# The first attention in batches of four heads, with p turned by block moves and VectorE instead of TensorE

## The reference: what is computed

```
h = rmsnorm(x, g_pre)
q, k, v, z = split(h @ w_in_a)
s = q k^T * scale + slope * distance          # masked to the window
p = exp(s - m) ; denominator = sum(p) + exp(sink - m)
o = p v / denominator
x = x + rmsnorm((o * silu(z)) @ w_out_a, g_post)
...
sh1, sc1, gt1, sh2, sc2, gt2 = silu(c) @ w_ada + b_ada
```

## Time and profile before

| | |
|---|---|
| median of 3 runs | 1768.04 us (1767.06 to 1768.81) |
| the profiled execution | 1767.72 us, its span 1766.0 us |
| TensorE busy | 1754.1 us, 99% of the span |
| VectorE busy | 1268.7 us, 72% |
| ScalarE busy | 882.5 us, 50% |
| GpSimd busy | 204.2 us, 12% |
| iterations 0, 1 and 2 of the first attention | 55.86, 55.87 and 55.87 us |
| granted TensorE clock | 0.999 of full speed |

### The profile page before, as it was taken

One profiled execution on the slowest core, in us unless ns is written; L12 is line 12 of the kernel. 1 busy time (PEld: TensorE's weight loads), 2 busy tenths in 40 slices (PEclk: granted clock), 3 DMA queues, 4 the chain that ended last, 5 costly groups with the idle time before them and its releaser, 6 DMA issues.

```text
span 1766.0 us, 24968 instructions
## 1 busy us (share of the span) xinstructions
PE 1754.1 (99%) x8130; PEld 1443.7 (82%) x8130; DVE 1268.7 (72%) x1649; ACT 882.5 (50%) x1235; POOL 204.2 (12%) x377
## 2 busy tenths in 40 slices
PE   9999999999999999999999999999999999999998
PEld 7777778887888888888888888888888888888886
DVE  5787779777988788777678768777775655554455
ACT  6876684545444354444445455444444444444443
POOL 1111101010233332410001101000000000000000
PEclk9999999999999999999999999999999999999999
DMA  9987778555798898898998958999997765555554
GB/s 339 301 296 254 249 259 311 202 165 173 238 269 292 271 293 274 269 322 287 320 311 299 322 171 267 319 310 311 319 292 238 237 216 193 194 194 191 192 194 138
DMA packets 201711, 454.29 MB, mean 257 GB/s; under 512 B 20160, under 2 KB 31408, under 8 KB 201264
## 3 DMA queue, kind: packets, MB, share of 16 engines
q1 hardware_dynamic: 168080, 343.28, 59.8%
q0 software_dynamic: 33424, 110.19, 18.8%
q10 hardware_dynamic: 144, 0.03, 0.0%
HBM read 434.03 MB, written 12.06 MB: 253 GB/s over the span
## 4 chain that ended last, share of the span: by engine, by line
PE 95%; DVE 2%; DMA 1%; ACT 1%; issue 0%; SPq 0%; DVEq 0%; ACTq 0%
PE bank L1684 30%; PE bank L1686 30%; PE bank L1685 30%; DMA raw<-in_w_in 1%; PE bank L1850 1%; PE bank L1730 1%; PE bank L1840 1%; DVE w_lo L1070 0%; PE bank L1942 0%; PE bank L1831 0%; PE bank L1828 0%; DVE x L1097 0%; PE bank L1710 0%; DMA raw<-in_w_in_a 0%; ACT y L661 0%
## 5 line engine op out<-in xcount | busy, mean ns | idle before, releaser
L1070 DVE TENSOR_TENSOR w_lo<-raw,w_hi 128x1024 fp32r<-128x1024 f32 x605 | 732.7, 1216 | 430.6 <-ACT w_hi L657 429.9
L657 ACT ACTIVATE w_hi<-raw 128x1024 fp32r<-128x1024 f32 x605 | 634.3, 1050 | 745.9 <-PE bank L1686 649.3
L1684 PE MATMUL bank<-w_hi,h_hi 128*128 128x512 f32 x2272 | 891.0, 392 | 2.0 <-DVE w_lo L1180 1.5
L1686 PE MATMUL bank<-w_hi,h_lo 128*128 128x512 f32 x2272 | 884.7, 389 | 0.0
L1685 PE MATMUL bank<-w_lo,h_hi 128*128 128x512 f32 x2272 | 884.4, 389 | 0.0
L1684 PEld LDWEIGHTS bank<-w_hi,h_hi 128*128 128x128 f32 x2272 | 426.5, 188 | 95.3 <-issue 5.8
L1686 PEld LDWEIGHTS bank<-w_hi,h_lo 128*128 128x128 f32 x2272 | 426.5, 188 | 89.6
L1685 PEld LDWEIGHTS bank<-w_lo,h_hi 128*128 128x128 f32 x2272 | 426.6, 188 | 86.6
L541 POOL DMA_DIRECT2D ada_raw<-in_w_ada x160 | 85.3, 533 | 745.4 <-DVE acc_a L1077 523.1
L1077 DVE SCALAR_TENSOR_TENSOR acc_a<-ada_raw,cond,acc_a 128x1024 f32<-128x1024 f32 x112 | 143.2, 1279 | 6.0 <-DMA ada_raw<-in_w_ada 6.0
L1077 DVE SCALAR_TENSOR_TENSOR acc_b<-ada_raw,cond,acc_b 128x1024 f32<-128x1024 f32 x48 | 61.4, 1278 | 0.0
(11 more groups left out here) (211 smaller groups left out, 929.8 us busy)
## 6 DMA issues: line engine op xcount, KB each, us to landing
raw<-in_w_ff SPq DMA_DIRECT2D x256, 512.0 KB, 4.6
raw<-in_w_in SPq DMA_DIRECT2D x176, 512.0 KB, 5.0
ada_raw<-in_w_ada POOLq DMA_DIRECT2D x160, 512.0 KB, 5.8
raw<-in_w_in_a SPq DMA_DIRECT2D x69, 512.0 KB, 5.2
ada_more<-in_w_ada POOLq DMA_DIRECT2D x32, 512.0 KB, 6.1
raw<-in_w_out_a SPq DMA_DIRECT2D x32, 512.0 KB, 5.8
raw<-in_w_o SPq DMA_DIRECT2D x32, 512.0 KB, 5.1
raw<-in_w_moba SPq DMA_DIRECT2D x16, 512.0 KB, 5.8
```

Of the source, the lines that this page charges most:

```text
L657: act.activation(used(w_hi, turn, s), used(raw, turn, s), ACT.Copy).then_inc(hi_ready, 1)
L1070: dve.tensor_tensor(used(w_lo, turn, s), used(raw, turn, s), used(w_hi, turn, s).bitcast(F32), ALU.subtract).then_inc(lo_ready, 1)
L1684: pe.matmul(out_ap, hi, rhs_hi, start=start, stop=False)
L1686: return pe.matmul(out_ap, lo, rhs_hi, start=False, stop=stop)
```

## The change

It touches iterations 0 to 2 of the first attention (the last group of heads keeps its way, with other counts in its waits).

- TensorE: the scores of four heads are made together, into banks 4 to 7, after slots 2 and 5 (`SLOTS_SCORES`); the outputs of four heads are made together, after slots 11 and 14 (`SLOTS_OUT`). The products that turned p (`turn_pair`) are gone from these iterations.
- ScalarE: Exp writes p in blocks of 32 columns into one of two buffers (the first 1536 columns of `post_gain`, or the new `p1_blk`). The copies of turned p are gone. The outputs of four heads are kept by one copy of 128x512 each.
- GpSimd: for each batch 16 DMAs move the blocks to a second place (`sums_r`, or the first columns of `x`), behind a wait for the four Exps. The loads of `w_ada` stand around them in its list, four ahead instead of two.
- VectorE: scores of a batch in the two slots behind TensorE's; four turns of 128x384 in slots 11 and 14 ahead of the split; the slots of the `w_ada` units are other ones.
- `x`, of which columns are overwritten, is loaded again (2 MB) after iteration 2.

The pieces of the diff below are, in this order, tables, buffers, GpSimd, ScalarE, VectorE and TensorE.

```diff
-STEPS = (2, 4, 6, 8, 10, 12)
+SLOTS_SCORES, SLOTS_BACK, SLOTS_OUT = (2, 5), (11, 14), (11, 14)
-ADA_ROWS_0, ADA_GAIN_0 = (4, 5, 6, 7), tuple(range(8, 16))
-ADA_ROWS, ADA_GAIN = (0, 1, 2, 4), (6, 8, 9, 10, 11, 13, 14, 15)
+ADA_ROWS_0, ADA_GAIN_0 = (2, 5, 5, 5), (8, 9, 9, 10, 13, 13, 15, 15)
+ADA_ROWS, ADA_GAIN = (1, 1, 2, 5), (8, 8, 9, 10, 13, 13, 15, 15)
...
+        p1_blocks = (p_blk, p1_blk[:, :])
+        p1_backs = (p_back, x[:, 0, 0:HEADS_BATCH * MASK_W])
+        p1_heads = (p1_t[:, 0, :], p1_t[:, 1, :], post_gain[:, 4 * MASK_W:5 * MASK_W], norm_rows[:, 0:MASK_W])
...
+            def move_heads1(i, b):
+                pool.wait_ge(p1_ready, i * GROUP_A + (b + 1) * HEADS_BATCH + 2)
+                if i:
+                    pool.wait_ge(p1_t_ready, (2 * i - 1 + b) * HEADS_BATCH)
+                for q in range(QUADS):
+                    for r in range(QUADS):
+                        move_p(pool, p1_blocks[b], p1_backs[b], p1_moved[b], q, r)
-            with pool.Fori(0, CHUNKS - 1) as i:
-                load_ahead(i, range(12))
+            for i in range(CHUNKS - 1):
+                load_units(i, range(4, 5 if i == 0 else 7))
+                move_heads1(i, 0)
+                load_units(i, range(5 if i == 0 else 7, 8))
+                move_heads1(i, 1)
+                load_units(i, range(8, 16))
+            pool.wait_ge(p1_t_ready, 2 * (CHUNKS - 1) * HEADS_BATCH)
+            for t in range(T):
+                pool.dma_start(x[:, t, :], x_in[t * P:(t + 1) * P, :]).then_inc(x_again, 16)
...
+            def batch_slot(i, n):
...
+                for b, at in enumerate(SLOTS_SCORES):
+                    first = b * HEADS_BATCH
+                    if n == at + 1:
+                        for k in range(2):
+                            attn1_exp_blocks(i, first + k)
+                            bias(i, first + k + 2)
+                    if n == at + 2:
+                        for k in range(2, 4):
+                            attn1_exp_blocks(i, first + k)
+                    if n == at + 3 and b == 0:
+                        for k in range(2):
+                            bias(i, HEADS_BATCH + k)
...
+            def turn_p1(i, b):
+                dve.wait_ge(p1_moved[b], i * MOVES + MOVES)
+                dve.wait_ge(o1_ready, i * PAIRS_A + 2 * b + 2)
+                returned = p1_backs[b].rearrange("p (i h b d) -> p h b i d", i=QUADS, h=HEADS_BATCH, b=3)
+                for k in range(HEADS_BATCH):
+                    dve.transpose(p1_heads[k], returned[:, k]).then_inc(p1_t_ready, 1)
+            def batch_slot(i, n):
+                here = [b * HEADS_BATCH + 2 * half for b, at in enumerate(SLOTS_SCORES) for half in range(2) if n == at + 1 + half]
+                for j in here:
+                    attn1_scores(i, j)
+                if n in SLOTS_BACK:
+                    turn_p1(i, SLOTS_BACK.index(n))
+                split(i * 2 + TURN_ZQ + n // UPT, n % UPT + AHEAD)
+                for j in here:
+                    attn1_scores(i, j + 1)
...
+            def scores1_batch(i, b):
...
+                pe.wait_ge(s1_masked, i * GROUP_A + b * HEADS_BATCH + 2)
...
+            def outs1_batch(i, b):
+                pe.wait_ge(p1_t_ready, i * GROUP_A + (b + 1) * HEADS_BATCH)
+                pe.wait_ge(s1_masked, i * GROUP_A + GROUP_A + 2)
```

More of the change, by code:

```diff
@@ new lines, in keep_batch @@
+            def keep_batch(i, b):
+                act.wait_ge(o1_ready, i * PAIRS_A + 2 * b + 4)
+                act.activation(o_t[:, 2 * b:2 * b + 2, :], two(banks[SCORES + b][:, :]), ACT.Copy).then_inc(o1_kept, 2)
+            def batch_slot(i, n):
+                if n == 0:
+                    for j in range(2):
+                        bias(i, j)
+                if n == 1:
+                    turn_q1(i)
+                for b, at in enumerate(SLOTS_SCORES):
[10 more added lines that the diff above has]
+                            bias(i, HEADS_BATCH + k)
+                if n == SLOT_SUMS:
+                    sink_share(i)
+                    z_sigmoid(i, i * 2 + TURN_ZQ)
+                if n == SLOTS_OUT[0] + 1:
+                    keep_batch(i, 0)
@@ L1090, in add_residual @@
             def add_residual(r, t, y):
+                if r == 1 and t == 0:
+                    dve.wait_ge(x_again, 32)
                 n = 2 * ((r - 1) * T + t)
@@ L1256, in set_heads, with attn1_scores @@
                 dve.tensor_copy(sink_cur[:, :], sink_sc[:, bass.ds(i * GROUP_A, GROUP_A)]).then_inc(heads_cur, 1)
-            def attn1_scores(i, j):
+            def attn1_scores(i, j, last=False):
                 h = i * GROUP_A + j
+                scores = banks[SCORES + j % (2 if last else HEADS_BATCH)]
                 dve.wait_ge(bias_ready, h + 1)
                 dve.wait_ge(s1_ready, h + 1)
-                dve.wait_ge(p1_turned, i * PAIRS_A + j // 2 + 1)
+                if last and j >= 2:
+                    dve.wait_ge(p1_turned, j // 2)
+                else:
+                    dve.wait_ge(p1_ready, h + 1)
                 if j == 0:
```

130 lines of the change are left out of this document (88 added, 42 removed).

## The result

The changed kernel takes 1787.74 us (median of 4 runs, 1786.61 to 1788.41), the kernel before 1768.28 beside it: ratio 1.0113, 95% interval 1.0100 to 1.0125. The forecast was 1781.0, range 1773 to 1796. The profiled execution took 1788.41 us, its span is 1786.7.

A forecast was written before the change was run, and what follows sets the result against it. TensorE's own work was taken as the bound (busy 99% of the span). Waits of 21.9 us against 8.9 saved gave +13.0, so 1767.72 + 13.0 = 1780.7, against the median 1781.0; range 1773 to 1796.

The forecast's parts named there:

- First waits: TensorE's output products wait for VectorE's first turns: 7.4 us in iteration 0, 5.0 in iterations 1 and 2.
- The turned heads: End of VectorE's list up to the first turns: there 33.4 us after TensorE's first score.
- TensorE's own way: TensorE's work from its first score until it needs the first turned heads: 28.4 us.
- Second waits: TensorE waits for VectorE's second turns, 1.5 us more in each iteration.
- Saved: TensorE's turning products removed and gaps made fewer: 2.96 us per iteration, 8.9 for three.
- the price of scores and outputs in fours: In TensorE's gaps, a pair's scores take 0.86 us and its outputs 0.80; their number stays.
- The clock: Rival: 5 us waits drop TensorE's clock; 1.2 us per iteration, +3.6 (1784.6), or about +20 (1801); chance 0.15.
- From first to second turned heads: VectorE's list between the two sets of turns, with splits, gate, heads and w_ada units: 11.5 us.
- The second load of x: Last group's w_ada loads stand behind x loaded again: 0 to 2 us, taken as 0.
- the loads come late: Rival: weight and w_ada loads land late beside the moves; +3 (1784) or about +18 (1799); chance 0.20.
- The cover that I named: VectorE's backlog covers the moves ahead of the turns; with that gone, 4 us of cover would be left.
- The chain was not covered: Rival: batches overlap better, VectorE five us shorter before the turns, only the saved 8.9 counts: 1759.1; chance 0.12.

The follow-up runs named there:

- e11: e10 without its 32 moves of p per iteration (a probe, its attention is another one): 1757.66 us, ratio to before 0.9944.
- e1: Changed kernel with VectorE taking both scores of a slot ahead of the slot's split of h: 1772.58 us, ratio to before 1.0031.
- e6: Changed kernel with new places of w_ada's units alone, and iteration 0's loads divided as in the others: 1776.93 us, ratio to before 1.0056.
- e3: Changed kernel without the moves of p, VectorE turning blocks in place (a probe, another attention): 1787.36 us, ratio to before 1.0110.
- e2: Changed kernel with TensorE computing 20 unread products per iteration where it waits for the first turns: 1780.97 us, ratio to before 1.0075.
- e4: Changed kernel with the second load of x placed later, its halves among a later group's w_ada loads: 1789.55 us, ratio to before 1.0121.
- e8: Changed kernel loading again only the part of x that the moves overwrite (0.75 MB), same place: 1784.87 us, ratio to before 1.0097.
- e10: e9 with w_ada's units placed anew, mostly in later slots, in all three iterations: 1767.66 us, ratio to before 0.9999.
- e9: Changed kernel with e1's order, e6's places of w_ada's units and e8's smaller load of x: 1763.77 us, ratio to before 0.9979.
- e12: e9 with the first w_ada unit of iteration 0 in slot 2 instead of slot 0: 1761.60 us, ratio to before 0.9967.
- e13: e12 with iteration 0's fourth gain unit in slot 10 instead of slot 9: 1761.17 us, ratio to before 0.9966.

## Why the prediction was right, and where its sum was short

The sign, the main mechanism (TensorE waits twice per iteration for VectorE's turns) and the places were right; the sum (+13.0) was 7.7 short of the profiled span's +20.7, and the largest loss that it left out is the clock's. Term by term, with e11's 52.07 us as an iteration without waits or clock loss:

- **First waits: forecast 7.4, 5.0, 5.0, came 7.2, 5.5, 5.5.** In iteration 0 6.03 at the turns and 1.2 for w_lo, as the text allowed. The turned heads were forecast 33.4 us behind TensorE's first score and came at 33.4; TensorE's own way was 28.0 instead of 28.4. e1 and e6 showed the two levers of this list, its order and the units in it; e3 excluded the moves.
- **Second waits: forecast 1.5 each, came 1.23, 1.23, 1.22.** With the clock held (e2) they are 1.6: the slow products behind the first wait eat 0.4 of the second. That the six waits add up to the forecast 21.9 is luck: two first waits were forecast 0.5 too short each, the other four waits 0.2 to 0.3 too long.
- **Saved: forecast 8.9, came 11.4** (3 x (55.87 - 52.07)). The term that was mis-sized is the price of scores and outputs in fours, taken over from single pairs: 2 x 0.86 for a batch's scores, 2 x 0.80 for its outputs. They take 1.51 and 1.45 (e1: 121.60 to 123.11, 151.29 to 152.74), 0.36 less per batch, 0.72 per iteration, or 2.2 of the 2.5.
- **The clock: forecast 0, came 7.1.** What is left of the iterations: 17.6 - 21.9 + 11.4. This is the largest error, and a step that the prediction had wrong: it priced a wait at its length alone. The mechanism stood as a rival at 0.15 and 1.2 us per iteration; it came in every iteration, at 2.2 to 2.5. The rival put the slow stretch into a big unit and let it hide behind the second wait; in truth the output products come first (1.3), a good two us of big products follow, and only 0.4 hides. The second turns don't stand still meanwhile: a slow TensorE frees ScalarE's split later, and VectorE waits for that split on its way to them. From first to second turned heads VectorE takes 13.3 us in iteration 1, with this wait, and 11.5 in e2, where it is gone (forecast 11.5):

```profile
167.76 1.23 DVE L1126 TENSOR_TENSOR w_lo<-raw,w_hi 128x1024 fp32r<-128x1024 f32 x1 [1.66 <-ACT w_hi L679]
```

  e2 gets 6.0 of the 7.1 back: its iterations hold 179.96 us, of which 156.21 are bare, 13.6 the 60 products and 9.0 waits; 1.1 is left. The trace of before held no long wait, so it couldn't show this; the price of a wait on TensorE should have been its length and a share for the clock.
- **The second load of x: forecast 0 of a range 0 to 2, came 1.7.** I looked at who reads x and at the w_ada loads behind it, not at the weights that land beside 2 MB (e4, e8).
- **Ahead of iteration 0: 1.5**, not forecast and not the change's; that stretch varies by 2.3 over the thirteen traces.

Sum: 21.9 - 11.4 + 7.1 + 1.7 + 1.5 = 20.8, against 20.7. The saving that was too small and the clock that was left out cancel by 2.5 of 7.1, so the 1781.0 was nearer than its terms deserved.

Of the rivals, that the loads come late did not happen in the changed kernel; it did in e10, where the cover was spent. The cover that I named, 4 us once the backlog is gone, was in the right place and for the wrong reason: the moves themselves landed in time, the weights beside them didn't. The chain was not covered, as forecast; e9, e12 and e13, in which it nearly is, are other kernels.

What stays open: why e4's and e8's iterations (64.1 to 61.4) are 0.2 to 1.1 us longer than the changed kernel's at nearly the same waits; the clock's return differs between executions, and no run holds it fixed there. Nor was it tried to space the moves apart on GpSimd, which e10 and e13 point to.

## What to carry over

Where a bound engine has to wait for a chain on two others, write the chain out as a list in order and time it; averages left VectorE 5 us per iteration, and the order took them away. Price a wait on TensorE of several microseconds at its length and some 2 us more (1.5 to 2.6 behind waits of 2.6 to 6.0 in these kernels), and look who loads beside a transfer that is moved, at the place it leaves and at the one it comes to. A transfer that is covered stays cheap only as long as the slack around it does: the same moves cost nothing in one schedule and 10 us in a tighter one.
